# Modulation products of a two-layer encoder step: four 32-column groups side by side, most of them hosted inside the input projections

## The reference, cut to what matters

```python
mod = jnp.einsum('bd,de->be', jax.nn.silu(c), lw['ada_w']) + lw['ada_b']    # 1024 -> 6144
sh1, sc1, g1, sh2, sc2, g2 = [m[:, None, :] for m in jnp.split(mod, 6, axis=-1)]
h = rms_norm(x, lw['norm_mix_g']) * (1 + sc1) + sh1
z = jnp.einsum('btd,dn->btn', h, lw['w_in'])                                # 1024 -> 5322
...                                                                         # three mixers on parts of z
x = x + g1 * (merged @ lw['w_out'])
h = rms_norm(x, lw['norm_ffn_g']) * (1 + sc2) + sh2
x = x + g2 * f                                                              # f: SwiGLU or experts of h
```

## Time and profile before

| | |
|---|---|
| median of three runs | 2545.38 us (2542.48 to 2548.31) |
| the profiled execution, its own time | 2540.93 us |
| span from its first to its last instruction | 2539.1 us |
| PE busy | 2376.3 us (94% of the span) |
| DVE, ACT, POOL busy | 761.7, 579.2, 300.5 us |
| share of the chain that ended last: PE | 92% |

### The profile page before, as it was taken

How to read it: one execution, slowest core, us unless ns; L and a number is a source line. 1 busy time by engine, 2 the same in 40 slices (tenths; PEclk the granted TensorE clock), 3 DMA queues, 4 the chain that set the end, 5 groups by cost and what they waited for, 6 DMA issues and landing times.

```text
span 2539.1 us, 40187 instructions
## 1 busy us (share of the span) xinstructions
PE 2376.3 (94%) x16529; PEld 2115.6 (83%) x16531; DVE 761.7 (30%) x1561; ACT 579.2 (23%) x1158; POOL 300.5 (12%) x194
## 2 busy tenths in 40 slices
PE   6989899899959999999989899899989999999995
PEld 3479799776859999996479799666869999999995
DVE  2013490453433333332013580453430000000014
ACT  2042422131142222211042422231241111111111
POOL 2023343000210000000023332000210000000001
PEclk9989999896979999999989999896999999999998
DMA  6722222230243223225721232000266888777883
GB/s 223 240 82 65 85 83 83 66 106 15 77 120 83 64 81 100 84 65 175 237 69 55 86 99 67 13 1 25 79 213 202 247 261 267 247 231 232 244 283 114
DMA packets 333972, 328.04 MB, mean 129 GB/s; under 512 B 7659, under 2 KB 325593, under 8 KB 333305
## 3 DMA queue, kind: packets, MB, share of 16 engines
q1 hardware_dynamic: 326720, 303.41, 38.9%
q0 software_dynamic: 5888, 18.52, 2.2%
q10 hardware_dynamic: 1256, 4.60, 0.5%
HBM read 310.29 MB, written 26.16 MB: 133 GB/s over the span
## 4 chain that ended last, share of the span: by engine, by line
PE 92%; ACT 3%; DVE 2%; issue 1%; POOL 1%; DMA 1%; DVEq 0%; POOLq 0%; ACTq 0%; SPq 0%
PE ps L1235 16%; PE ps L882 16%; PE ps L1186 15%; PE ps L843 10%; PE ps L1214 7%; PE ps L817 7%; PE ps L798 5%; PE ps L1040 4%; PE ps L1024 3%; PE ps L1002 2%; PE ps L788 1%; PE ps L825 1%; ACT hT L1316 1%; PE ps L947 1%; PE ps L1163 1%
## 5 line engine op out<-in xcount | busy, mean ns | idle before, releaser
L1235 PE MATMUL ps<-hR,wR 128*128 128x272 f32 x2112 | 270.3, 291 | 31.2 <-DVE wR L1953 26.6
L882 PE MATMUL ps<-hH,slotsR 128*128 128x272 f32 x1536 | 293.7, 291 | 3.7 <-ACT oT L1385 3.7
L1235 PEld LDWEIGHTS ps<-hR,wR 128*128 128x128 f32 x2112 | 269.8, 191 | 31.8 <-DVE wR L1953 27.0
L882 PEld LDWEIGHTS ps<-hH,slotsR 128*128 128x128 f32 x1536 | 244.0, 190 | 4.4 <-issue 4.4
L674 POOL TENSOR_TENSOR slotsR<-slots,slotsR 128x1024 fp32r<-128x1024 f32 x64 | 154.5, 2435 | 699.2 <-ACT slotsR L1336 699.2
L843 PE MATMUL ps<-wz,hH 128*128 128x250 f32 (+1 forms) x720 | 206.7, 287 | 21.4 <-POOL slotsR L674 15.0
L882 PE MATMUL ps<-hL,slotsR 128*128 128x272 f32 x768 | 223.0, 290 | 0.0
L843 PE MATMUL ps<-slotsR,hH 128*128 128x250 f32 (+1 forms) x720 | 204.4, 284 | 0.0
L843 PE MATMUL ps<-wz,hL 128*128 128x250 f32 (+1 forms) x720 | 203.5, 283 | 0.0
L674 POOL TENSOR_TENSOR slotsR<-slots,wz 128x1000 fp32r<-128x1000 f32 x36 | 85.5, 2399 | 842.2 <-ACT wz L1336 842.2
L1186 PE MATMUL ps<-hg,slots 128*128 128x160 f32 x1280 | 177.3, 300 | 1.6 <-ACT hg L1476 0.6
(11 more groups left out here) (336 smaller groups left out, 3665.5 us busy)
## 6 DMA issues: line engine op xcount, KB each, us to landing
slots<-in_ada_w SPq DMA_DIRECT2D x48, 1024.0 KB, 5.2
slots<-in_w_in SPq DMA_DIRECT2D x24, 1024.0 KB, 5.2
slots<-in_w_in SPq DMA_DIRECT2D x18, 1000.0 KB, 5.0
slots<-in_moe_w_gate SPq DMA_DIRECT2D x16, 1024.0 KB, 6.2
slots<-in_moe_w_up SPq DMA_DIRECT2D x16, 1024.0 KB, 8.0
w_more<-in_moe_w_gate SPq DMA_DIRECT2D x16, 1024.0 KB, 5.5
w_more<-in_moe_w_up SPq DMA_DIRECT2D x16, 1024.0 KB, 8.0
w_more<-in_moe_w_down SPq DMA_DIRECT2D x16, 768.0 KB, 4.4
```

The source lines that it names most:

```text
L882: last = mm(ps[:, 2 * out_pair + a, 0:HALF], w[:, c], r[:, n], start=(k == i == 0), stop=(k == KD - 1 and i == 2))
L1235: last = mm(ps[:, 2 * out_pair + h, 0:HALF], wR[:, buf, a, k * P:(k + 1) * P], rhs(k, b)[:, c], start=(first and k == 0 and i == 0), stop= ...
```

## The change

The modulation work is cut into chunks of 512 columns, twelve a layer, numbered through (0 to 11 layer 0, 12 to 23 layer 1). A chunk comes as two transfers of 1 MB (four of the eight 128-row parts each). Its eight products go in two rounds of four: product `g` of a round has 32 stationary columns (2 of silu(c), 30 zeros) and writes PSUM partitions `32g` to `32g+31` of bank 5, so four different parts of the sum stand in four groups of partitions (`ada_rows`). ACT copies all 128 partitions (`ada_copy`), TensorE transposes four 128x128 pieces (`ada_columns`), and DVE adds up the four groups while it reads them (`ada_sum`).

Four chunks (`sh1`, `sc1` of layer 0) stay up front. The other eight of layer 0 and the first four of layer 1 follow after given tiles of layer 0's z stage, the last eight of layer 1 after tiles of layer 1's z stage (`ADA_AT`: the tile numbers of 45). Layer 1 has no modulation stage in front any more. Two further buffers take the transfers beside the z weights (`ada_x`, and `pp` as `ada_y`); the constant `poolm`, which lives in `pp`, is now loaded after the z stage. The z loops are written out instead of looped, and the rounding of the first gate block moves behind the z stage, since its target was lent to the chunks.

```diff
+AW = 512
+ADA_FIRST, ADA_LATER = 4, 8
+ADA_AT = [[1, 4, 8, 12, 16, 19, 23, 27, 31, 35, 39, 42], [6, 10, 14, 18, 23, 28, 34, 40]]
...
-        csil = sb("csil", [P, KD, 2])
+        csil = sb("csil", [P, KD, 32])
...
+        ada_places = [0, 1, 2, 3, 4, 5, 3, 4] + [(5, 3, 4)[i % 3] for i in range(4 * ADA_LATER + 2 * ADA_FIRST)]
...
+                def ada_fill(u):
...
+                    if ada_places[u] in ada_places[:u]:
+                        before = max(i for i in range(u) if ada_places[i] == ada_places[u])
+                        sp.wait_ge(ada_used, before + 1)
+                    dst = ada_slots[ada_places[u]].rearrange("p (k n) -> p k n", k=4)
+                    sp.dma_start(dst, src[:, (u % 2) * 4:(u % 2) * 4 + 4, c * AW:(c + 1) * AW])\
+                        .then_inc(ada_full[ada_places[u]], 16)
...
-                pe.wait_ge(v_ready, 2 * L + 1)
-                with pe.Fori(0, 6) as it:
-                    for j in range(4):
-                        landed(("ada", L), it, j)
...
+                def ada_rows(n, bank):
+
+                    if n:
+                        pe.wait_ge(ada_copied, n)
+                    for u in (2 * n, 2 * n + 1):
+                        pe.wait_ge(ada_full[ada_places[u]], ada_landed(u))
+                        for g in range(4):
+                            last = mm(ps[32 * g:32 * g + 32, bank, 0:AW], csil[:, (u % 2) * 4 + g, :],
+                                      ada_slots[ada_places[u]][:, g * AW:(g + 1) * AW], start=(u % 2 == 0), stop=(u % 2 == 1))
+                        last.then_inc(ada_used, 1)
+
+                def ada_columns(n):
+
+                    pe.wait_ge(ada_copied, n + 1)
+                    if n >= 2:
+                        pe.wait_ge(ada_summed, n - 1)
+                    for f in range(4):
+                        last = nc.tensor.transpose(ps[:, 6 + n % 2, f * P:(f + 1) * P], mrow[:, n % 2, f * P:(f + 1) * P], ident[:, :])
+                    last.then_inc(ada_done, 1)
...
+                            at = it * (ZBODY * TILES) + g
+                            if at in hosted:
+                                ada_rows(hosted[at], 5)
+                            if at - 1 in hosted:
+                                ada_columns(hosted[at - 1])
...
-                                elif isinstance(it, int):
-                                    proj_high(("gates", L), 0, 0)
...
+                act.wait_ge(ada_used, 2 * (max(hosted.values()) + 1))
+                proj_high(("gates", L), 0, 0)
...
+                    V.tensor_reduce(mod[:, 4 * c:4 * c + 4, :],
+                                    ps[:, 6 + n % 2, :].rearrange("p (f g s) -> p f s g", f=4, g=4)[:, :, 0:2, :], AX.X, ALU.add)\
+                        .then_inc(ada_summed, 1)
```

More of the change, by code:

```diff
@@ L327, in encoder_step @@
         oTf = oT[:, :, :].rearrange("p k n -> p (k n)")
-        mrow = oTf[0:2, 4 * NTOK:4 * NTOK + 1024].rearrange("p (j n) -> p j n", j=4)
+        mrow = oTf[:, 2816:2816 + 2 * AW].rearrange("p (j n) -> p j n", j=2)
+        place["gT_ada"] = (place["gT"][0] + ZBODY * KD * ZB * 4, SLOT * 4)
+        ada_x = sb("ada_x", [P, SLOT], over="gT_ada")
+        ada_y = pp[:, :, :, :].rearrange("p a b n -> p (a b n)")
+        ada_slots = [slots[:, i, :] for i in range(NSLOT)] + [ada_x[:, :], ada_y]
         score = oTf[:, 0:1312]
@@ L492, in proj_parts, with ada_chunk, ada_landed, ada_hosted @@
             return slotsR[:, 3 - j % 2, :], slotsR[:, j % 2, :], 2 * P
+        ada_places = [0, 1, 2, 3, 4, 5, 3, 4] + [(5, 3, 4)[i % 3] for i in range(4 * ADA_LATER + 2 * ADA_FIRST)]
+        def ada_chunk(n):
+            return (0, n) if n < ADA_FIRST + ADA_LATER else (1, n - ADA_FIRST - ADA_LATER)
+        def ada_landed(u):
+            return 16 * ada_places[:u + 1].count(ada_places[u])
+        def ada_hosted(L):
+            first = ADA_FIRST if L == 0 else ADA_FIRST + ADA_LATER + ADA_FIRST
+            return {at: first + i for i, at in enumerate(ADA_AT[L])}
         def moe_landed(n, b):
@@ L541, in _ @@
-                with sp.Fori(0, ZITER) as it:
-                    for j in range(ZBODY):
-                        fill(("z", L), it, j, [(cols(j, ZB), w_in[:, :, ds(it * (ZBODY * ZB) + j * ZB, ZB)])])
+                def ada_fill(u):
+                    layer, c = ada_chunk(u // 2)
+                    src = t_in["ada_w"][layer].rearrange("(k p) n -> p k n", p=P)
+                    if ada_places[u] in ada_places[:u]:
[4 more added lines that the diff above has]
+                        .then_inc(ada_full[ada_places[u]], 16)
@@ new lines, in _ @@
+                if L == 0:
+                    for u in range(2 * ADA_FIRST):
+                        ada_fill(u)
+                hosted = ada_hosted(L)
+                spots = sorted(hosted)
+                events = [(max(0, TILES * (b - 2)), 0, b) for b in range(ZITER * ZBODY)]
+                events += [(spots[(i - 3) // 2] + 1 if i >= 3 else 0, 1, i) for i in range(2 * len(spots))]
+                for _, kind, i in sorted(events):
+                    if kind == 0:
+                        it, j = divmod(i, ZBODY)
+                        if L == 0 and it == 0:
+                            sp.wait_ge(ada_used, j + 1)
+                        fill(("z", L), it, j, [(cols(j, ZB), w_in[:, :, i * ZB:(i + 1) * ZB])])
+                        continue
+                    if L and i == 0:
+                        sp.wait_ge(x_upd, xu(0, "ffn"))
+                    ada_fill(2 * hosted[spots[i // 2]] + i % 2)
@@ new lines, in ada_columns @@
+                def ada_columns(n):
[5 more added lines that the diff above has]
+                    last.then_inc(ada_done, 1)
+                if L == 0:
+                    for n in range(ADA_FIRST):
+                        ada_rows(n, 5)
+                        if n:
+                            ada_columns(n - 1)
+                    ada_columns(ADA_FIRST - 1)
@@ L830, in _ @@
+                hosted = ada_hosted(L)
+                for it in range(ZITER):
                     for j in range(ZBODY):
@@ L1339, in _, with ada_copy @@
                 root(2 * L)
[L1341 to L1344, removed]
+                def ada_copy(n, bank):
+                    act.wait_ge(ada_used, 2 * n + 2)
+                    if n >= 2:
+                        act.wait_ge(ada_done, n - 1)
+                    A(mrow[:, n % 2, :], ps[:, bank, 0:AW], ACT.Copy).then_inc(ada_copied, 1)
+                if L == 0:
+                    for n in range(ADA_FIRST):
+                        ada_copy(n, 5)
                 norm(2 * L, lambda k, s: scl[:, 0, k, s:s + 1],
-                     lambda k, s: mod[:, M_SH1 + k, s:s + 1], L + 1, split=True)
-                def z_blocks(it):
+                     lambda k, s: mod[:, M_SH1 + k, s:s + 1], 2 * L + 1, split=True)
+                hosted = ada_hosted(L)
+                for it in range(ZITER):
                     for j in range(ZBODY):
@@ L1580, in _, with ada_sum, ada_finish @@
                 stats(2 * L)
[L1582 to L1588, removed]
+                def ada_sum(n):
+                    layer, c = ada_chunk(n)
+                    dve.wait_ge(ada_done, n + 1)
+                    V.tensor_reduce(mod[:, 4 * c:4 * c + 4, :],
+                                    ps[:, 6 + n % 2, :].rearrange("p (f g s) -> p f s g", f=4, g=4)[:, :, 0:2, :], AX.X, ALU.add)\
+                        .then_inc(ada_summed, 1)
+                def ada_finish(layer, a, b, n):
+                    dve.wait_ge(ada_summed, n)
+                    bias = vecT[:, layer, V_ADAB + a:V_ADAB + b].unsqueeze(2).to_broadcast([P, b - a, 2])
+                    ch.link(V.tensor_tensor(mod[:, a:b, :], mod[:, a:b, :], bias, ALU.add))
+                    i, sc0, g0 = (0, M_SC1, V_NMIX) if a == 0 else (1, M_SC2, V_NFFN)
+                    gain = vecT[:, layer, g0:g0 + KD].unsqueeze(2).to_broadcast([P, KD, 2])
+                    V.scalar_tensor_tensor(scl[:, i], mod[:, sc0:sc0 + KD, :], 1.0, gain, ALU.add, ALU.mult).then_inc(mod_ready, 1)
+                if L == 0:
+                    for n in range(ADA_FIRST):
+                        ada_sum(n)
+                    ada_finish(0, 0, 16, ADA_FIRST)
                 for k in range(KD):
@@ L1614, in rope, with ada_hosted_sums @@
                         dve.wait_ge(rope_done, ropes[0])
+                hosted = sorted(ada_hosted(L).values())
+                early = [n for at, n in ada_hosted(L).items() if at < 4 * TILES]
+                def ada_hosted_sums(which):
+                    for n in which:
+                        ada_sum(n)
+                        if n == ADA_FIRST + ADA_LATER - 1:
+                            ada_finish(0, 16, 48, n + 1)
+                        elif n == 2 * ADA_FIRST + ADA_LATER - 1:
+                            ada_finish(1, 0, 16, n + 1)
+                        elif n == 2 * (ADA_FIRST + ADA_LATER) - 1:
+                            ada_finish(1, 16, 48, n + 1)
```

(2 more changed lines are left out.)

60 lines of the change are left out of this document (20 added, 40 removed).

## The result

The changed kernel takes **2419.8 us** (median of 4 runs, 2414.02 to 2420.99) where the kernel before takes 2543.93 us in the same set (2538.48 to 2548.31): ratio 0.9514, 95% interval 0.9497 to 0.9531, 124 us less. The forecast was 2427, in a range from 2410 to 2470. The profiled execution took 2420.24 us, its span is 2418.4 us.

The account below looks back on a forecast made before the run. TensorE's own sequence was taken as the bound, PE being on 92% of the chain. Terms -84 - 91.9 + 54 + 4 = -118 us from 2540.93 gave 2423, plus 4.4 for the median: 2427 us, range 2410 to 2470.

Parts of the forecast that it names:

- Four groups at once: Modulation chunk: four column groups run side by side, four steps, 1.77 us of products instead of 7.07; chance 0.70.
- the rivals: Chunk products: two at a time (2466 us, 0.14), one by one (2550, 0.09), every group empties the array (2604, 0.04).
- Twenty hosted chunks at 2.7 us, 54 us: z stages of both layers: each hosted chunk lengthens PE's work by 2.7 us, 54 us more for twenty.
- the change of form: Each chunk: switching between forms of products empties the array, taken as two times 158 ns, 0.32 us.
- waits at hand: Each hosted chunk in z: 0.1 us allowed for waits, part of the 2.7 us.
- Layer 1's front, 91.9 us: Before layer 1's norm: modulation stage goes whole, scaling starts 8.1 us after the sums, 91.9 us less.
- Layer 0's front, 84 us: Before layer 0's norm: four chunks stay, scaling starts at 51 us instead of 134.87, 84 us less.
- both limits fall together: Layer 0's front: the eighth transfer lands at about 48 us, DVE's `stats` ends at 47.3 us.
- Gate rounding, 2 us a layer: Behind each z stage: ACT's rounding now stands before the log forget steps, 2 us more a layer, 4 in all.
- No transfer late in z: z stages: chunk transfers issued 8 to 11 us ahead against 5.2 to land; chance of data late beyond cover 0.03.
- Sum: Whole kernel: -84 - 91.9 + 54 + 4 = -118 us against the profiled 2540.93 us, giving 2423 us.
- The 4.4 us that the forecast added for the median: Whole kernel: median before, 2545.38 us, is 4.4 us above the profiled execution, so 2423 became 2427 us.

Follow-up runs that it names:

- all three edits: Changed kernel plus gate rounding back inside z, two more front buffers, and DVE's chunk sums moved among the `stats` products: 2406.38 us, again 2406.85 against 2420.00.

## Why the prediction was right, step by step

- **Four groups at once**: right, and the rivals fell. It was a bet, put at 0.70: the trace of before had two row groups side by side and no column groups. The four first records start 6 to 7 ns apart (37.721 to 37.740 us). Products 1.85 us against 1.77 forecast. Two groups run 6.98 / 3.56 = 1.96 and four 6.98 / 1.85 = 3.77 times as fast as one, close to their number. By the 2.38 times that the Trainium skill (TensorE: Matmul & The Clock Gate, Part 3, Measured speedup) gives for three column groups (0.79 of the ideal, carried over to four), a chunk would take an estimated 2.23 us; four groups were faster than that, and three were not run. The rivals' prices hold too: 8.0 and 4.5 us a hosted chunk were forecast for one and two groups, 7.73 and 4.27 measured.
- **Twenty hosted chunks at 2.7 us, 54 us**: 2.53 in layer 0; in layer 1 (1292.97 - 1131.35) less (1413.09 - 1271.45) before, 20.0 us for eight, 2.50: together 50.3 us. Transposes 0.44 against 0.51, the change of form 0.22 against 0.32, waits at hand none. The copies of layer 1's last z tile, before and now:

```profile
1413.09 0.37 ACT z L1352
```

```profile
1292.97 0.04 ACT z L1411
```

- **Layer 1's front, 91.9 us**: the interval from sums to scaling is 8.1 us, as forecast.
- **Layer 0's front, 84 us**: 79.4. The scaling came at 55.51, not 51 us. 3.0 of the 4.5 us are the norm sums, which took 10.46 us instead of 7.58. The transfers were forecast well: the eighth landed 13.1 us after the sums (50.9 after 37.8), against 13.2 forecast (48 after 34.8). The other 1.5 us lie behind it. From its landing to the scaling it took 4.6 us instead of 3.0, because TensorE then ran at 1.2 GHz (0.51 in the window from 50 us on, above): the last half chunk took 1.94 us, where the half before it took 1.06 and the forecast had 1.0, and eight transposes 1.91. The sum had both stretches at the full clock. That both limits fall together was right, as the experiments above show.

```profile
47.67 1.06 PE L852 MATMUL ps<-slots,csil 128*32 128x512 f32 x8 [2.16 <-DMA slots<-in_ada_w]
...
50.97 1.94 PE L852 MATMUL ps<-ada_x,csil 128*32 128x512 f32 x8 [2.24 <-DMA ada_x<-in_ada_w]
```

- **Gate rounding, 2 us a layer**: 1.9 and 1.9.
- **No transfer late in z**: right, in layer 0 PE is busy without a gap at 189 GB/s (219 were estimated), and in layer 1 the chain between its first product and its last copy is PE alone.
- **Sum**: -79.4 + 30.3 + 1.9 - 91.8 + 20.0 + 1.9 = -117.1 against -118 forecast. The span fell by 120.7. The other 3.6 us lie behind the scores: 1.1 from layer 0's score products to layer 1's sums (886.0 against 887.1), 2.5 from layer 1's score products to the end. In the other kernels here, with the same code in both stretches, these spread from 881.0 to 887.1 and from 1113.4 to 1119.4, so the 3.6 are within what these stretches vary. That the sum lies within 1 us is partly luck: layer 0's front was forecast 4.5 us too short and the hosted chunks 3.7 us too dear. The 4.4 us that the forecast added for the median did not show, since here the median lies at the profiled execution.

## What to carry to other kernels

Products with few stationary columns can be split over the sum into column groups and run side by side at nearly the number of groups; what remains is a small fixed price for the transposes and the change of form. Hosting such work in a stage where TensorE is already busy hides its transfers, not its products, so cut the products first and then host. Where two limits fall within a microsecond of each other (a last transfer, a block of DVE work in front of small sums), moving one alone gains little: here 2.3 or 0.6 of the 5.9 us that both gained.

## What the runs showed of the hardware

Products of different column groups are not held in the order of the program: the experiment with the groups written one after the other ran them all from the first source, then all from the second, at no loss (1.9 us a chunk).

At the start of the program the granted clock is not the same from kernel to kernel, and not always from one execution of a kernel to the next. Windows of the changed kernel, and of the one with the gate rounding inside z:

```profile
28.00:30.00 2.00, 2.00 (x6) 1.53 (x5) 0.00 (x0) 2.00 (x5) 0.00 (x0) 0.50 0.35 129
```

```profile
28.00:30.00 2.00, 2.00 (x10) 1.68 (x9) 0.00 (x0) 2.00 (x5) 0.00 (x0) 1.00 0.15 52
```

In the first the norm sums begin at 1.2 GHz (0.50) and end at 37.79 us, in the second they run at 2.4 GHz and end at 34.31. All code up to there is the same. Before it PE was busy 4.98 of the 6 us from 20 us on in the one and 4.34 in the other. The kernel with all three edits had the sums in 9.02 us (0.50 in the window from 28 us on) in its first profile and in 7.57 us (1.00) in its second. In the profiles of the changed kernel and its variants the sums end between 34.1 and 37.9 us; what decides it stays open, and it is the larger part of the forecast's miss in layer 0.
